# Attention logits of two heads issued together on the two row halves of TensorE, and formed two steps ahead

## The reference

```python
# per block of 128 queries; 8 heads of 64
idx = top-256 keys by indexer score, causal          # the same keys for all heads
logits = q . k_sel / 8 + bias[bucket(t - s)]          # masked to s <= t
p = softmax(logits);  out = p @ v_sel
```

## Time and profile before

| | |
|---|---|
| time, median of 3 runs | 2257.06 us (2255.24 to 2257.71) |
| the profiled execution's own time | 2260.85 us |
| its span | 2259.2 us |
| TensorE busy | 2150.1 us, 95% of the span |
| DVE, ACT, POOL busy | 1066.2, 626.6, 332.1 us |
| granted TensorE clock, mean | 0.962 of full speed |

### The profile page before, as it was taken

How to read it: one execution, slowest core, us unless ns; L and a number is a source line. 1 busy time by engine, 2 the same in 40 slices (tenths; PEclk the granted TensorE clock), 3 DMA queues, 4 the chain that set the end, 5 groups by cost and what they waited for, 6 DMA issues and landing times. The chain is left out here.

```text
span 2259.2 us, 31153 instructions
## 1 busy us (share of the span) xinstructions
PE 2150.1 (95%) x12125; PEld 1900.5 (84%) x12125; DVE 1066.2 (47%) x2226; ACT 626.6 (28%) x1108; POOL 332.1 (15%) x294
## 2 busy tenths in 40 slices
PE   6999997999999999999979999999999999999997
PEld 4789997988888777677758997799988998889986
DVE  5589996344444330354455432633344333443345
ACT  4423221222332262334353321412112121121112
POOL 6512222322121222000112430000000000000000
PEclk9999998999999879998888999999999999999998
DMA  4202331222121133333353423210111101111102
GB/s 141 79 22 84 124 102 60 78 84 67 50 64 39 63 118 94 135 136 127 107 194 123 140 60 114 75 38 28 48 56 57 38 19 57 57 39 39 37 1 87
DMA packets 144140, 173.82 MB, mean 77 GB/s; under 512 B 9689, under 2 KB 120831, under 8 KB 143487
## 3 DMA queue, kind: packets, MB, share of 16 engines
q1 hardware_dynamic: 136158, 148.14, 20.1%
q0 software_dynamic: 7840, 23.67, 3.0%
HBM read 127.38 MB, written 44.40 MB: 76 GB/s over the span
## 5 line engine op out<-in xcount | busy, mean ns | idle before, releaser
L855 PE MATMUL ring<-n_hi,piece_hi 128*128 128x352 f32 (+1 forms) x1320 | 442.2, 335 | 1.0 <-DVE n_whole L1661 1.0
L857 PE MATMUL ring<-n_hi,piece_lo 128*128 128x352 f32 (+1 forms) x1320 | 429.8, 326 | 0.0
L856 PE MATMUL ring<-n_lo,piece_hi 128*128 128x352 f32 (+1 forms) x1320 | 429.7, 326 | 0.0
L1239 ACT ACTIVATE arena<-ring 128x352 f32<-128x352 f32 (+7 forms) x368 | 153.6, 438 | 636.0 <-PE ring L857 451.9
L2194 POOL TENSOR_TENSOR piece_lo<-piece_whole,piece_hi 128x1024 fp32r<-128x1024 f32 (+2 forms) x71 | 164.0, 2310 | 742.9 <-ACT piece_hi L1252 742.8
L855 PEld LDWEIGHTS ring<-n_hi,piece_hi 128*128 128x128 f32 (+1 forms) x1320 | 252.6, 191 | 7.8 <-issue 5.6
L856 PEld LDWEIGHTS ring<-n_lo,piece_hi 128*128 128x128 f32 (+1 forms) x1320 | 252.8, 192 | 0.6
L857 PEld LDWEIGHTS ring<-n_hi,piece_lo 128*128 128x128 f32 (+1 forms) x1320 | 251.6, 191 | 0.5
L1749 DVE TENSOR_SCALAR_CACHE_REDUCE arena<-arena 128x384 uint8<-128x384 f32 (+6 forms) x224 | 190.7, 875 | 1.4 <-DVE arena L1749 0.2
L856 PE MATMUL ring<-h_lo,gate_hi 128*128 128x352 f32 x528 | 170.7, 323 | 6.0 <-issue 6.0
L855 PE MATMUL ring<-h_hi,gate_hi 128*128 128x352 f32 x528 | 171.9, 325 | 0.0
(11 more groups left out here) (278 smaller groups left out, 3702.7 us busy)
## 6 DMA issues: line engine op xcount, KB each, us to landing
piece_whole<-w_in SPq DMA_DIRECT2D x54, 512.0 KB, 3.6
projected_rows<-arena SPq DMA_DIRECT2D x44, 528.0 KB, 2.7
arena<-projected_rows SPq DMA_DIRECT2D x12, 1056.0 KB, 5.0
gate_whole<-w_ffn_gate SPq DMA_DIRECT2D x11, 1024.0 KB, 5.2
up_whole<-w_ffn_up SPq DMA_DIRECT2D x11, 1024.0 KB, 5.1
down_whole<-w_ffn_down SPq DMA_DIRECT2D x11, 1024.0 KB, 4.8
arena<-projected_rows SPq DMA_DIRECT2D x16, 528.0 KB, 3.5
arena<-x_prompt SPq DMA_DIRECT2D x16, 512.0 KB, 5.3
```

The costliest lines, as they stand in the source:

```text
L855: pe.matmul(out, lhi, rhi, start=first, stop=False)
L856: pe.matmul(out, lhi, rlo, start=False, stop=False)
L857: return pe.matmul(out, llo, rhi, start=False, stop=last)
L1239: evacuates(act.activation(dst, src, ACT.Copy, scale=scale), *key)
```

## The change

TensorE issues the logits of an even and an odd head together, the chunks of the two in turns, so that neighbouring matmuls use different row halves and different PSUM buffers. Pair p holds units 2p and 2p + 1 and is issued at the start of every even step, one pair ahead. `lg_full` now counts pairs. DVE forms logits two steps ahead, after the copy and the mask step instead of before them; the mask steps move from heads 1 to 6 to heads 0 to 5. ACT's exponential goes two ahead, POOL's `near` three ahead.

```diff
@@ SP
-                    sp.wait_ge(lg_full, u + 1)
+                    sp.wait_ge(lg_full, (u + 1) // 2)
-            sp.wait_ge(lg_full, len(UN))
+            sp.wait_ge(lg_full, len(UN) // 2)
@@ TensorE
-            def qk(u):
-                b, h = UN[u]
+            def qk_pair(p):
+
+                b, h = UN[2 * p]
                 if h == 0:
                     pe.wait_ge(qb_in[b % 2], 16 * (b // 2 + 1))
-                if u >= 2:
-                    pe.wait_ge(lg_used, u - 1)
-                p0 = 64 * (h % 2)
+                if p >= 1:
+                    pe.wait_ge(lg_used, 2 * p)
                 L = P * (b + 1)
                 for c0 in range(0, L, 512):
                     c1 = min(L, c0 + 512)
-                    ins = pe.matmul(lgt[u % 2][:, c0:c1], qb[b % 2][p0:p0 + 64, h // 2, :],
-                                    kdT[p0:p0 + 64, h // 2, c0:c1], start=True, stop=True)
+                    for e in range(2):
+                        p0 = 64 * e
+                        ins = pe.matmul(lgt[e][:, c0:c1], qb[b % 2][p0:p0 + 64, h // 2, :],
+                                        kdT[p0:p0 + 64, h // 2, c0:c1], start=True, stop=True)
                 ins.then_inc(lg_full, 1)
...
-            qk(0)
+            qk_pair(0)
             for u, (b, h) in enumerate(UN):
-                if u + 1 < len(UN):
-                    qk(u + 1)
+                if u % 2 == 0 and u + 2 < len(UN):
+                    qk_pair(u // 2 + 1)
@@ ACT
             exp(0)
+            exp(1)
...
-                if u + 1 < len(UN):
-                    exp(u + 1)
+                if u + 2 < len(UN):
+                    exp(u + 2)
@@ DVE
-                v.wait_ge(lg_full, u + 1)
+                v.wait_ge(lg_full, u // 2 + 1)
...
             logits(0)
+            logits(1)
             for u, (b, h) in enumerate(UN):
                 if u >= 1:
                     norm_head(u - 1)
-                if u + 1 < len(UN):
-                    logits(u + 1)
...
-                if b >= 1 and 1 <= h <= 6:
-                    mask_step(b - 1, h - 1)
+                if b >= 1 and h <= 5:
+                    mask_step(b - 1, h)
+                if u + 2 < len(UN):
+                    logits(u + 2)
@@ POOL
-            near(0)
-            near(1)
+            for u in range(3):
+                near(u)
             for u, (b, h) in enumerate(UN):
-                if u + 2 < len(UN):
-                    near(u + 2)
+                if u + 3 < len(UN):
+                    near(u + 3)
```

## The result

The changed kernel takes 2205.57 us (median of 4 runs, 2202.2 to 2211.91) against 2256.15 before (four runs; three of them gave the 2257.06 that the forecast started from): a ratio of 0.9775, 95% interval 0.9763 to 0.9787, so 50.6 us less. The forecast was 2217.7 with a range of 2208 to 2230: right in direction and on what a pair costs, with a gain of 39.4 us that was 11.2 too small, and the time is outside the range by 2.4. The profiled execution of the changed kernel took 2211.91 us (span 2210.2), the slowest of its four; it is set against the 2260.85 us of before, 48.9 us.

The account below looks back on a forecast made before the run. TensorE was taken to bound the prompt-attention stage. Terms 33.2 - 0.6 - 1.5 + 8.3 gave a gain of 39.4 us, so a median of 2217.7 us against 2257.06, range 2208 to 2230.

Parts of the forecast that it names:

- I take the slot of a pair as the slot of one product: Query-key products: two heads issued together take one head's time, 1.92 us in block 7.
- the bound by TensorE: Prompt-attention steps: a microsecond of TensorE work removed shortens the end by one, if other engines' chains still fit.
- The term of the slots: Query-key products up to unit 60: 68.4 us before, 35.1 as pairs, a gain of 33.2 us.
- the formula: A query-key product's slot in block b: 0.213 x (b + 2) us, covering each 128 keys plus load and drain.
- the rival with a warm tail: Last four units: the clock stays up, gaining 15.1 us instead of 8.3, time 2211; chance 0.20.
- If it falls 7.4 us into step 60 again: Last four units: the clock falls to half as before, so they take 24.4 us, a gain of 8.3.
- the full clock's case: Last four units with the clock staying up: 17.6 us, a gain of 15.1.
- The rival with a chance of 0.20: Last four units: the clock stays up, gain 15.1 us instead of 8.3, time 2211; chance 0.20.
- Loss 1.5: Logits and exponential made later, behind copy and mask step: TensorE stalls at projection banks, 1.5 us in all.
- The chain for block 6: Block 6, head 2: bank evacuated at 8.95 us of the step, wanted at 8.68, a stall of 0.3 to 0.4.
- Loss 0.6: Start of the stage: pair (2,3) delays the first transpose by 1.0 us, 0.43 already counted, so 0.6 lost.
- only shifts: Gate logits and sample attention after the stage: released by its end and moved in time, with no gain counted.

Follow-up runs that it names:

- e1: The changed kernel with pairs undone, one query-key product in each step, two units ahead, new engine orders kept: 2247.18 us, ratio 0.9953 to the kernel before.
- e5: The kernel before, with DVE copying the transposed bank ahead of the next unit's logits from unit 60 on: 2248.47 us, ratio 0.9959.
- e3: The changed kernel, but in units 60 and 61 DVE forms the logits two ahead before the copy of the transposed bank: 2218.3 us, ratio 0.9825.
- e4: The changed kernel with DVE's mask step behind the logits two ahead instead of ahead of them: 2204.89 us, ratio 0.9764.
- e6: The changed kernel run again unaltered, for another profile and more runs: 2203.59 us, ratio 0.9757.
- e2: The changed kernel with the even head's chunks all ahead of the odd head's, instead of in turns: 2204.14 us, ratio 0.9763.
- e8: The changed kernel with mask step last, three projection groups ahead of unit 0 and the other 57 in units 7 to 63: 2198.11 us, ratio 0.9729.
- e7: The changed kernel with the mask step last and the 60 projection groups in units 4 to 63 instead of 0 to 59: 2203.53 us, ratio 0.9756.

## Why the prediction was wrong in size

- **"I take the slot of a pair as the slot of one product"** held to 0.01 us, and so did the bound by TensorE. Between the first transpose and unit 60 the products took 67.9 us before (59 of them) and 34.7 after (29 pairs), 33.2 less; the sum has 33.6 for the same ones, since it counts the pair (2,3), 0.43, that stands ahead of the first transpose.
- **The term of the slots was mis-sized all the same**, because the formula was fitted to slots alone. A product also lengthens its neighbours: the P·V ahead of it takes 1.60 against 1.51, and the transposes behind it 0.74 against 0.69. An odd step now has no product in it, and saves 0.15 us there in block 6; over all steps P·V and transposes gained 4.2 us. The sum had nothing for this, and so the rival with a warm tail (2211) and the low end of the range (2208) lay too high as well. e1, with 4.5 us for it in its forecast, came out at 41.6 against 39.6. That the change of row layout is the reason is my reading; no run separates it.
- **"If it falls 7.4 us into step 60 again"** was the failed step, with the largest part: the last four units gained 15.1 us, not 8.3. The working of the full clock's case was right (17.6 us was forecast and 17.6 was measured); I chose the other case, taking the moment of the fall from the distance to the last projection group. e5 shows that it depends on what the steps hold: with the copy first, the old kernel's clock stays up until late in unit 62. e3 shows the other direction. The rival with a chance of 0.20 was the case, though narrowly: the clock fell 17.8 us after unit 60 began, when 17.6 were enough.
- **"Loss 1.5" for the moved logits** was 0.9. The places came out as unit 33 (0.27, forecast 0.5), unit 43 (0.39, forecast none: its scan took 2.44 us, where 2.02 had been read before), unit 51 (0.05, forecast 0.35) and the pair behind unit 27 (0.17, not forecast). e4 shows that the mask step ahead of the logits is the cause of all but unit 33's. The chain for block 6 as it is written adds up to 8.8 us, not 8.95; it leaves a gap between ACT's operations unnamed (0.17 us in the rows of unit 42).
- **"Loss 0.6" at the start**, counted as a transpose 1.0 later: 0.9.
- From the first transpose to unit 60, then: products 33.2, P·V and transposes 4.2, stalls -0.9, and 1.1 from the projection groups (the first one took 5.01 us against 6.57, more of it at full clock; in e6 it took 6.30, so this is mostly the execution's; the others took 0.5 more). That makes 37.6; 37.7 was measured, and the forecast had 32.1.
- **"only shifts"** for what follows: 0.9 less in the profiled pair of executions; in e2, e4 and e6 it is 5 to 6.5 less. The gate logits, partly at full clock, give 1.0 to 1.7 of that (12.7 to 13.4 us instead of 14.4); the rest comes in pieces up to 1.1 ms further on and wasn't traced. The same kernel's two profiles differ by 9.1 us in span: 5.2 ahead of the first logits and 5.2 behind the turned block, less 1.3 between. So single terms can be tested in a single profile only within the stage between these two.

In sum, the gain was 11.2 us over the forecast: 6.8 from the clock in the last four units and 5.6 up to unit 60, of which 4.2 are the neighbours of the products. The remaining -1.2 is made of the later search (-3.8), the end of the program (0.9), the start (0.1) and the distance of the two profiled executions from their medians (1.6).

## What to carry to other kernels

Two products with 64 rows each, on opposite halves of the array and into different PSUM banks, cost the time of one; if they are kept apart by other work, put them side by side, in any order. Price an instruction by the step with and without it, not by its own slot: its neighbours' slots change with it. Where an in-order engine works for TensorE in a stretch with no cover, let it do first what TensorE waits for next; here the order of a copy and a reduction in four steps kept the clock up some 10 us longer, and was worth about 10 us without any other change (e5). And ask of each engine what stands ahead of the one operation that the others wait for: in e8 a weight piece on POOL cost 4 us of the gain.

## What the runs showed of the hardware that I had not expected

- Matmuls on one row half overtook earlier ones on the other: with four matmuls of the even head ahead in the program, both halves started at 713.68 (e2).
- The gate logits, 24 matmuls with 16 rows, busy without a pause, had a granted clock of 0.54 and 0.66 in e7 and e8, though it was 1.00 when they began: it fell 1 us after their start in e7 and 3 us after it in e8. In the first profile of the changed kernel it had fallen before they began.
- The end of the mask search moved by 5.2 us between two executions of the same kernel (first logits at 367.30 in e6 and at 372.51). Half of that, 2.5 us, is that the search began later (128.6 and 131.1). The 224 counting passes took 195.8 and 196.0 us; the other 2.6 lie in operations on four or three elements, some of which took up to 2.44 us instead of 0.23.
